# The first gate/up panels of the first FFN cut by feature chunk instead of by unit, in a fused two-layer conditioned decoder trunk

## The reference, cut to what matters

```python
c_act = jax.nn.silu(c)
mod = (c_act @ ada_w[l] + ada_b[l]).reshape(b, N_MOD, d)[:, :, None, :]
modulate = lambda t, i: rms_norm(t, norm_g[l, i]) * (1.0 + scale(i)) + shift(i)

h = modulate(x, 0)
x = x + 0.5 * gate(0) * swiglu(h, ffn_wg[l, 0], ffn_wu[l, 0], ffn_wd[l, 0])
def swiglu(h, wg, wu, wd):
    return (jax.nn.silu(h @ wg) * (h @ wu)) @ wd
```

## Time and profile before

| | |
|---|---|
| median of 3 runs | 1281.35 us (1281.32 to 1281.73) |
| the profiled execution | 1281.08 us |
| its span, first to last instruction | 1279.3 us |
| TensorE busy | 1234.3 us (96%) |
| VectorE busy | 965.5 us (75%) |
| ScalarE busy | 546.9 us (43%) |
| DMA, mean over the span | 229 GB/s |

### The profile page before, as it was taken

The page is one execution under the profiler, slowest core; times in us unless marked ns, Lnnn a source line. Parts: engine busy times, 40 slices in busy tenths (PEclk is TensorE's granted clock), DMA queues, the critical chain, the costliest instruction groups (busy, mean ns, idle before and its releaser), DMA issues.

```text
span 1279.3 us, 13844 instructions
## 1 busy us (share of the span) xinstructions
PE 1234.3 (96%) x5440; PEld 957.3 (75%) x5448; DVE 965.5 (75%) x1341; ACT 546.9 (43%) x576; POOL 2.2 (0%) x5
## 2 busy tenths in 40 slices
PE   3999999999999999999999999999999999999997
PEld 2588887766776887888878888876676678888885
DVE  5698886699997576988668888668999866644443
ACT  3343434532344555344355433354323564634431
POOL 0000000000000000000000000000000000000000
PEclk9999999999999999999999999999999999999999
DMA  9989994444233539889747889545532335455540
GB/s 375 416 317 373 375 377 177 184 179 166 100 113 118 191 111 377 345 342 356 301 170 276 343 344 356 193 162 204 188 133 99 132 132 196 167 197 189 193 177 34
DMA packets 52913, 293.44 MB, mean 229 GB/s; under 512 B 6640, under 2 KB 6896, under 8 KB 27120
## 3 DMA queue, kind: packets, MB, share of 16 engines
q1 hardware_dynamic: 51120, 289.38, 60.4%
q10 hardware_dynamic: 1728, 3.17, 0.7%
HBM read 291.45 MB, written 1.07 MB: 229 GB/s over the span
## 4 chain that ended last, share of the span: by engine, by line
PE 90%; DVE 3%; DMA 3%; ACT 2%; issue 1%; SPq 0%; DVEq 0%
PE ps L329 24%; PE ps L331 24%; PE ps L330 24%; PE ps L348 12%; DMA raw<-in_weights 2%; PE ps L515 1%; PE ps L396 1%; PE ps L537 1%; DMA ada_raw<-in_ada_w 1%; DVE hF L1084 1%; PE ps L526 0%; PE ps L485 0%; ACT L715 0%; DVE w_lo L997 0%; PE ps L380 0%
## 5 line engine op out<-in xcount | busy, mean ns | idle before, releaser
L997 DVE TENSOR_TENSOR w_lo<-raw,w_hi 128x2048 fp32r<-128x2048 f32 x176 | 401.0, 2286 | 40.8 <-ACT w_hi L709 40.5
L709 ACT CAST w_hi<-raw 128x2048 fp32r<-128x2048 f32 x176 | 334.5, 1910 | 163.7 <-PE ps L331 82.9
L329 PE MATMUL ps<-w_hi,hA_hi 128*128 128x512 f32 (+1 forms) x992 | 397.7, 401 | 2.9 <-DVE hA_lo L997 2.9
L331 PE MATMUL ps<-w_hi,hA_lo 128*128 128x512 f32 (+1 forms) x992 | 385.2, 388 | 0.0
L330 PE MATMUL ps<-w_lo,hA_hi 128*128 128x512 f32 (+1 forms) x992 | 384.6, 388 | 0.0
L329 PEld LDWEIGHTS ps<-w_hi,hA_hi 128*128 128x128 f32 x992 | 187.4, 189 | 46.6 <-issue 11.9
L330 PEld LDWEIGHTS ps<-w_lo,hA_hi 128*128 128x128 f32 x992 | 187.7, 189 | 38.5 <-issue 3.3
L331 PEld LDWEIGHTS ps<-w_hi,hA_lo 128*128 128x128 f32 x992 | 187.2, 189 | 38.9
L1186 DVE SCALAR_TENSOR_TENSOR work<-conv_in,par,work 128x256 f32<-128x256 f32 x480 | 193.7, 478 | 0.0
L1012 DVE SCALAR_TENSOR_TENSOR product<-ada_raw,c_bc 128x1024 f32<-128x1024 f32 x144 | 171.6, 1220 | 15.6 <-DMA ada_raw<-in_ada_w 15.2
L348 PE MATMUL ps<-raw,hF 128*128 128x512 f32 x384 | 171.6, 598 | 5.5 <-ACT hF L734 5.5
(11 more groups left out here) (120 smaller groups left out, 741.8 us busy)
## 6 DMA issues: line engine op xcount, KB each, us to landing
raw<-in_weights SPq DMA_DIRECT2D x200, 1024.0 KB, 4.8
ada_raw<-in_ada_w SPq DMA_DIRECT2D x144, 512.0 KB, 6.7
gate_bc<-gate_scratch ACTq DMA_DIRECT2D x6, 512.0 KB, 6.3
x<-in_x_tok SPq DMA_DIRECT2D x1, 1024.0 KB, 7.4
out_tok<-xn_h SPq DMA_DIRECT2D x4, 256.0 KB, 2.2
c_bc<-in_c_row SPq DMA_DIRECT2D x1, 512.0 KB, 4.4
c_bc<-in_g_row SPq DMA_DIRECT2D x1, 512.0 KB, 5.6
mask_all<-in_mask SPq DMA_DIRECT2D x1, 416.0 KB, 16.3
```

The costliest lines, as they stand in the source:

```text
L329: nc.tensor.matmul(out_ap, stat[0], mov[0], start=start, stop=False)
L331: return nc.tensor.matmul(out_ap, stat[1], mov[0], start=False, stop=stop)
L709: nc.scalar.copy(w_hi[:, s % HI, :], raw[:, p % RAW, :]).then_inc(hi_done, 1)
L997: return nc.vector.tensor_tensor(dst, whole, hi_part.bitcast(F32), ALU.subtract)
```

## The change

**Panels.** Panels 0 to 7 now hold one feature chunk each (chunk k in panel k) of units 0 to 3, so each carries 4 x 512 columns. Only panels 0 and 1 are whole (`FIRST_WHOLE` 4 to 2); 2 to 7 are split. The down panels of units 0, 1, 2, 3 are 8, 9, 10, 13; panels 11 and 12 are unit 4.

**Banks.** Units 0 to 3 accumulate in banks 0/1, 2/3, 4/5, 6/7. The down results need banks 0 to 3, so `down(0, 0)` comes after units 0 and 1 have left them.

**Start.** `x` comes in two halves, the parameters in two parts. VectorE sums the squares of the first half of `x` and scales it, ScalarE does both for the second half. After that the modulation goes chunk by chunk: two blocks, `finish_norm` of one chunk, and in the same step the split of weight panel k and of the activations of chunk k.

**Order after it.** The two streams below are written out for units 0 to 3; from unit 4 on the old loop runs. The 48 later blocks are spread over panels 10 to 31 (before: 8 to 31).

```diff
-FIRST_WHOLE = 4
+FIRST_WHOLE = 2
+FIRST_UNITS = 4
 def ada_before(p):
-    if p < 3:
-        return 16
+    if p < mix_base(0):
+        n = ADA_AT[1] - ADA_AT[0]
+        return ADA_AT[0] + max(0, min(n, -(-n * (p - 9) // 22)))
...
+            sp.dma_start(x[:, 0, :], x_in[:, 0, :]).then_inc(x0_load, 16)
+            sp.dma_start(x[:, 1, :], x_in[:, 1, :]).then_inc(x1_load, 16)
+            sp.dma_start(ident_sb[:], ident).then_inc(ident_in, 16)
+            load_ada(2)
+            sp.dma_start(par[:, 0:C_CW], params[:, 0:C_CW]).then_inc(norms_in, 16)
             load(0)
+            for k in range(1, KC):
+                load_ada(2 * k + 2)
+                load(k)
...
+            def k_step(k, u, tt):
+                t, c = slice(tt * P, (tt + 1) * P), slice(512 * u, 512 * u + 512)
+                out_ap = ps[:, unit_bank(0, u) + tt, :]
+                if is_whole(k):
+                    return nc.tensor.matmul(out_ap, hF[:, k, t], raw[:, k % RAW, c], start=(k == 0), stop=False)
+                hi, lo = parts(k)
+                return three(out_ap, (hA_hi[:, k, t], hA_lo[:, k, t]), (hi[:, c], lo[:, c]), k == 0, k == KC - 1)
+            def first_units():
+                for k in range(KC - 2):
+                    ready(k)
+                    if is_whole(k):
+                        pe.wait_ge(hk_done, k + 1)
+                    else:
+                        pe.wait_ge(h_lo_done, k + 1)
+                    for u in range(FIRST_UNITS):
+                        if k == 0 and u == 2:
+                            pe.wait_ge(xT_done, 4)
+                        for tt in range(TT):
+                            mm = k_step(k, u, tt)
+                    mm.then_inc(panel_done, 1)
+                for u in range(FIRST_UNITS):
+                    for tt in range(TT):
+                        for k in range(KC - 2, KC):
+                            if u == 0 and tt == 0:
+                                ready(k)
+                                pe.wait_ge(h_lo_done, k + 1)
+                            mm = k_step(k, u, tt)
...
+                    if u in (1, 2):
+                        turn(0, u - 1, (0, 1))
+                pe.wait_ge(mid_lo_done, unit(0, 1))
...
+                    first_units()
+                    down(f, 0, 0)
+                    down(f, 0, 1)
+                    turn(f, 2, (0, 1))
+                    down(f, 1, 0)
+                    down(f, 1, 1)
+                    turn(f, 3, (0, 1))
+                    down(f, 2, 0)
+                    down(f, 2, 1)
...
+            def first_norm():
+                for i in range(4):
+                    act_e.wait_ge(hT_done, i + 1)
+                    nc.scalar.copy(hF[:, 2 * i:2 * i + 2, :], cols(4 + i)).then_inc(xT_done, 1)
+                    if i == 0:
+                        first_full(0)
+                preload(ACT.Silu)
+                first_hi(0)
+                for k in range(1, KC):
+                    first_full(k)
+                    first_hi(k)
+                    hi(k)
+            def first_full(k):
+                act_e.wait_ge(xT_done, k // 2 + 1)
+                act_e.wait_ge(mods_done, k + 1)
+                nc.scalar.activation(hF[:, k, :], hF[:, k, :], ACT.Identity, bias=modb[:, 0, k:k + 1],
+                                     scale=gs[:, 0, k:k + 1]).then_inc(hk_done, 1)
+            def first_hi(k):
+                act_e.wait_ge(hk_done, k + 1)
+                nc.scalar.copy(hA_hi[:, k, :], hF[:, k, :]).then_inc(h_hi_done, 1)
...
+            def first_lo(k):
+                dve.wait_ge(h_hi_done, k + 1)
+                minus(hA_lo[:, k, :], hF[:, k, :], hA_hi[:, k, :]).then_inc(h_lo_done, 1)
...
+            norm_scale(0, 0)
+            ada_units(0, 1)
+            norm_recip(0, 1)
+            ada_units(1, 2)
+            finish_norm(0, 0, 1)
+            for k in range(1, KC):
+                ada_units(2 * k, 2 * k + 2)
+                finish_norm(0, k, 2 * k + 1)
+                if k == 1:
+                    first_lo(0)
+                lo(k)
+                first_lo(k)
```

More of the change, by code:

```diff
@@ L255, in h_at, with mods_at, unit_bank, mid_parts @@
         def h_at(n, tt, b):
-            return 4 * n + (2 * b + tt if n == 0 else 2 * tt + b) + 1
+            return KC + 4 * (n - 1) + 2 * tt + b + 1
         def unit(f, j, tt=0):
             return (NJ + 1) * f + j + tt + 1
-        def mods_at(g, b=1):
-            return b + 1 if g == 0 else g + 2
+        def mods_at(g):
+            return KC + g
+        def unit_bank(f, j):
+            return 2 * j if f == 0 and j < FIRST_UNITS else 4 + 2 * (j % 2)
+        def mid_parts(f, j):
+            return (mid2_hi, mid2_lo) if f == 0 and j in (1, 3) else (mid_hi, mid_lo)
         def acc(half, tt):
@@ L424, in ffn @@
                 if f == 0:
[L425 to L431, removed]
+                    first_units()
[7 more added lines that the diff above has]
+                    down(f, 2, 1)
                 else:
                     two_groups(g[:2], n, (gu(0), gu(1)), lambda: norm_turn(n, 1), lambda: turn(f, 0, (0, 1)))
[L434 to L438, removed]
+                    down(f, 0, 0)
+                    down(f, 0, 1)
+                for j in range(2 if f else FIRST_UNITS, NJ - 1):
                     both(g[j][0], hA, 0, gu(j))
-                    turn(f, j - 1, (0, 1))
+                    if f or j > FIRST_UNITS:
+                        turn(f, j - 1, (0, 1))
                     both(g[j][1], hA, 1, gu(j))
@@ L983, in _ @@
             preload(ACT.Sqrt)
-            for tt in range(TT):
-                norm_square(0, tt)
-                norm_std(0, tt)
+            norm_std(0, 0)
+            norm_square(0, 1)
+            norm_std(0, 1)
+            act_e.wait_ge(rstd_done, 2)
+            for half in range(2):
+                c = slice(half * 512, half * 512 + 512)
+                nc.scalar.activation(xn_h[:, 1, c], x[:, 1, c], ACT.Copy, scale=rstd[:, 1:2]).then_inc(xn1_done, 1)
             for l in range(DEPTH):
@@ L1018, in finish_norm @@
             def finish_norm(g, b, q):
-                first, last = (0, KC) if b is None else (4 * b, 4 * b + 4)
+                first, last = (0, KC) if b is None else (b, b + 1)
                 o = C_LAYER * (g // 3) + C_ADAB + (g % 3) * 3 * KC
@@ L1395 @@
             f = 2 * l + s
+            first = []
             for j in range(NJ):
@@ L1399 @@
                 pa, pb = gate_panels(f, j)
-                panels[pa], panels[pb] = k_halves(gu)
+                if f == 0 and j < FIRST_UNITS:
+                    first.append(rows(gu))
+                else:
+                    panels[pa], panels[pb] = k_halves(gu)
                 panels[down_panel(f, j)] = rows(a["ffn_wd"][l, s][c]).reshape(P, PW)
+            if f == 0:
+                for k in range(KC):
+                    panels[k] = np.concatenate([r[:, k] for r in first], axis=1)
         w, b = a["w_in"][l], mix_base(l)
```

170 lines of the change are left out of this document (99 added, 71 removed).

## The result

The changed kernel takes 1298.88 us in the median (1296.74 to 1299.26, 4 runs) against 1281.34 us for the kernel before in the same set of runs: a ratio of 1.0137, 95% interval 1.0122 to 1.0152. It is slower by 17.5 us; 16.6 were forecast. The profiled execution took 1298.53 us, its span is 1296.5 us.

What follows compares the result with a forecast made beforehand. TensorE sets the time once the first FFN runs, so only the head counts: the next panel starts at 104.9 us, 106.7 with clock, against 90.1. That adds 16.6 to 1281.1, giving 1297.7 us; range 1290 to 1301.5.

Steps and rivals of the forecast that it cites:

- first matmul: Start of TensorE's matmuls, set by panel 0's landing: 13.7 us instead of 24.4, 10.7 us sooner.
- period of a chunk: Chunk loop from chunk 2 on: 8.28 us per chunk, against 5.45 us of split matmuls on TensorE.
- chunk 7 starts: Chunk loop: chunk 7 is ready for TensorE at 69.9 us, after a 7.6 us gap.
- head in all: First FFN up to the panel after `down(1)` and turn 3: +16.6 us against the kernel before, clock included.
- The ring: Chunk loop: ScalarE and VectorE wait for each other, 8.28 us a chunk; TensorE idles some 18 us.
- The second wait: Before `down(2)`: VectorE's `hidden(3)`, seven blocks and three `lo` delay `mid_low(2)`; TensorE stands 10.1 us.
- The clock: TensorE's matmuls run at 1.2 GHz behind long gaps: +1.8 us after the 7.6 us gap, +1.8 before `down(2)`.
- the rival that gave 1305 us: Chunk loop: TensorE's clock stays low from chunk to chunk, 10.3 us a chunk; 1305 us, chance 0.05.
- What I costed at nothing: Work behind the head: VectorE and DMA keep up, and panels 9 and 10, held back by block 22, cost zero.
- the ring of six panels: Panel buffering taken as cover for late panels 9 and 10; without it each would cost its lateness.
- the faster rival's 1267.4 us: Chunk loop and `down(2)`: both engines' handovers are hidden, so TensorE and DMA bind; 1267.4 us, chance 0.05.
- that rival's 1279.3: Fourth case: the ring is hidden but `down(2)` still waits, 1267.4 + 10.1 + 1.8 = 1279.3 us, chance 0.03.

Runs made afterwards that it cites:

- e1: Changed kernel with ScalarE's rounding of weight panel k (`hi(k)`) moved ahead of `first_full(k)` in the chunk loop; 1291.25 us, 1.0086 of the kernel before.
- e2: Changed kernel with `mid_low(2)` moved right behind `hidden(3)`, ahead of VectorE's blocks and splits; 1288.21 us, 1.0062 of the kernel before.
- f1: Changed kernel with VectorE's wait for the second part of the parameters moved behind the first FFN; 1298.57 us, 1.0141 of the kernel before.
- e3: Changed kernel with the edits of e1 and e2 together; 1281.01 us, 1.0004 of the kernel before.
- f2: Changed kernel with the edits of e3 and f1 together; 1273.37 us, 0.9947 of the kernel before.
- f3: f2 with the three blocks and the split of panel 10 (`ada_lo(10)`) moved ahead of `hidden(3)`; 1270.37 us, 0.9924 of the kernel before.
- e4: Changed kernel with eleven unneeded float32 matmuls put into TensorE's gap before `down(2)`; 1296.50 us, 1.0121 of the kernel before.

## Why the prediction was right

| step | forecast | measured |
|---|---|---|
| first matmul | 13.7 us | 13.95 |
| VectorE waits for `w_hi` | 2.8 us, six times | 2.96 to 2.98, six times |
| period of a chunk | 8.28 us | 8.27 to 8.29 |
| chunk 7 starts | 69.9 us | 69.99 |
| idle before it, and the four gaps before that | 7.6; 10.2 | 7.34; 7.48 |
| `down(2)` starts, idle before it | 104.9; 10.1 us | 105.14; 10.18 |
| low clock behind the two long gaps | 1.8 + 1.8 us | 1.3 + 2.5 |
| head in all | +16.6 us | +17.7 |

**The ring** was right in mechanism and size. Its period is a sum of both engines' work (2.86 us of ScalarE, 5.42 of VectorE) because each waits for the other once per chunk, and e1 shows it: one instruction moved, 5.22 us in place of 8.28. The four gaps before chunk 7 are shorter than forecast, 7.5 us in place of 10.2: chunk 2 ended 0.4 us later (its first matmul starts at 29.47 as forecast, but its second only at 30.10), a record lasts longer than the 0.227 us by which I had counted, so that each listed gap is some 0.2 us under mine, and one chunk of 24 matmuls, that at 45.15, ran in part at the low clock, which took 1.6 us from the gap behind it (0.98 against 2.57). That was idle time only: the period stayed.

**The second wait** was right. Gap less what remained in e2, plus the clock, is 10.1 - 1.0 + 1.8 = 10.9 us by my numbers with a remainder of 1.0; e2 measured 9.6 with one of 1.24 and the new gap of 1.14. One sentence ahead of the prediction is wrong: in the kernel before, not two blocks and one split but four blocks and two splits stand between the product of unit 2 (73.94 us) and its `mid_low`. They cost nothing there, since they run before the turn; behind the turn nothing is in the way but ScalarE's `mid_high` (VectorE in the timeline of the kernel before):

```profile
84.91 0.69 DVE L997 TENSOR_TENSOR mid_lo<-ps,mid_hi 128x512 fp32r<-128x512 f32 x1 [1.10 <-ACT mid_hi L771]
```

In the changed kernel it is all ten instructions that start only once turn 2 is through.

**The clock.** The sum took 1.8 us for each long gap. The first long gap was followed by six slow matmuls (69.99 to 72.69, 2.70 us where six at 0.227 take 1.4, so 1.3 lost), the second by twelve. The terms were off in opposite directions and their sum was 3.9 against 3.6, which is in part luck: the second term alone was 0.7 us short, most of the 1.1 us by which the head was missed. Of the four chunks ahead of chunk 7 only the one at 45.15 has matmuls 0.43 us apart (up to 48.80), and they ate idle time; those behind the gaps of 1.37 and 0.98 us ran at the full rate, and behind that of 2.56 us only three matmuls follow. So the clock did not stay low from chunk to chunk, and the rival that gave 1305 us fell. The Trainium skill (TensorE: Matmul & The Clock Gate, section "HAM oscillation") tells of a low clock in every chunk of a loop whose compute is shorter than the wait for the next data. The prediction applied that to all five gaps, but the condition does not hold for four of them: 5.45 us of matmuls against under 3 us of waiting. It holds only at chunk 7, with three matmuls ahead of 7.34 us of waiting, and there the trace agrees.

**What I costed at nothing, with the wrong cover.** "I cost all of it at nothing; the cover is the ring of six panels": block 22 holds back not only panels 9 and 10 in SyncE's queue but the second part of the parameters, and all of VectorE's stream behind the chunk loop waits for those. I had moved the load in the queue without asking who waits for it, nor how long it takes to land behind the others (11.9 us in e1). The zero was right (f1), but by the cover of the two-engine ring, and without it the price is 7.3 us (e3 to f2). So the faster rival's 1267.4 us left out a third thing that had to be repaired; f3, with all of them repaired, came to 1270.4, 3 us from it. The same wait is most of the reason why e1, which hides the ring but not `down(2)`, came to 1291.3 and not to that rival's 1279.3.

## What to carry to other kernels

When two engines that each work through their own stream in order wait for each other in one step of a loop, and each stands still while the other works, the period is the sum of their work and not the longer of the two. Put the instruction that needs only a transfer ahead of the one that needs the partner. And when a wait costs nothing, write down what hides it: here an unrelated stall hid a late load worth 7 us, so that repairing the first showed only half of its gain until the second was repaired too.

## What the runs showed that I had not expected

Gaps of the same length did not always lower the clock. Within the chunk loop of e2 all 24 matmuls behind a gap of 2.57 us, at 37.09, ran at the full rate, and seven of those behind the next, 2.59 us at 45.38, came 0.43 us apart, from the fourth on. (That of 2.56 us at 61.72 in the changed kernel tells nothing: only three matmuls follow.) TensorE in the mixing layer of the changed kernel (timeline), behind 2.52 us of idling:

```profile
417.45 1.04 PE L630 MATMUL ps<-ident_sb,work 128*128 128x128 f32 x4 [2.52 <-DVE work L1307]
418.15 0.78 PE L349 MATMUL ps<-w_hi,hA_hi 128*128 128x512 f32 x1
418.72 0.63 PE L350 MATMUL ps<-w_lo,hA_hi 128*128 128x512 f32 x1
```

and at the same place of e4, behind 2.52 us as well:

```profile
415.25 0.66 PE L632 MATMUL ps<-ident_sb,work 128*128 128x128 f32 x4 [2.52 <-DVE work L1309]
415.66 0.48 PE L349 MATMUL ps<-w_hi,hA_hi 128*128 128x512 f32 x1
415.98 0.39 PE L350 MATMUL ps<-w_lo,hA_hi 128*128 128x512 f32 x1
```

Matmuls start 0.43 us apart in the first, 0.23 in the second. At chunk 7 it was the same: in f2 twelve slow matmuls followed a gap of 3.64 us,

```profile
55.21 0.77 PE L349 MATMUL ps<-w_hi,hA_hi 128*128 128x512 f32 x1 [3.64 <-DVE hA_lo L1108]
55.78 0.63 PE L350 MATMUL ps<-w_lo,hA_hi 128*128 128x512 f32 x1
```

and in e3 none followed one of 3.61 us:

```profile
55.03 0.47 PE L349 MATMUL ps<-w_hi,hA_hi 128*128 128x512 f32 x1 [3.61 <-DVE hA_lo L1108]
55.33 0.40 PE L350 MATMUL ps<-w_lo,hA_hi 128*128 128x512 f32 x1
```

The same instructions in the same order, at nearly the same time and behind nearly the same gap, thus differ by up to 2.5 us from one execution to the next. That would explain why kernels with several gaps of 2.5 to 3.6 us spread over 2.4 to 3.9 us from run to run (the changed kernel, e1, e3, e4, f1, f2), and f3 over 0.8; since only one execution of each was profiled, it is argued and not shown. e2, with three gaps of 2.56 to 2.59 us, spread over only 0.8, so it can't be the gaps' number alone. What decides whether the clock falls behind such a gap stays open; behind the gaps of 7 and 10 us it fell every time they were profiled.
